# One core, a hybrid encoder layer: the convolution's split halves and the output weights change places in SBUF, with another chunk order and another list of priorities

## The reference, cut to what matters

```
h = rms_norm(x); u = h @ w_in                       # 1024 -> 2560 columns: q, k, v (512 each), conv (1024)
a = neighbourhood_attention(q, k, v, rpb)           # 8 heads x 64, window of rows x 16 columns, relative bias
c = conformer_conv(uc)                              # GLU, depthwise conv of width 31, layer norm, swish
m = concat(rms_norm(a), rms_norm(c))
x = x + m @ w_out                                   # 1024 x 1024
x = x + hier_moe(rms_norm(x))                       # top-1 group of 4, top-2 of 8 experts in it, 32 experts
y = rms_norm(x)
```

## Time and profile before

| | us |
|---|---|
| median of 3 runs | 912.96 (912.54 to 914.18) |
| the profiled execution | 913.56 |
| its span in the trace | 911.7 |

### The profile page before, as it was taken

One profiled execution on the slowest core, in us unless ns is written; L12 is line 12 of the kernel. 1 busy time (PEld: TensorE's weight loads), 2 busy tenths in 40 slices (PEclk: granted clock), 3 DMA queues, 4 the chain that ended last, 5 costly groups with the idle time before them and its releaser, 6 DMA issues.

```text
span 911.7 us, 15694 instructions
## 1 busy us (share of the span) xinstructions
PE 848.1 (93%) x5814; PEld 571.5 (63%) x5815; DVE 374.4 (41%) x697; ACT 242.3 (27%) x482; POOL 139.2 (15%) x288
## 2 busy tenths in 40 slices
PE   3989999999979999989999879999999999999984
PEld 2879977777757878965555445555555555555531
DVE  5399979796374535541111101111111111111146
ACT  5223216545675222101111111111111111111122
POOL 4200010000000001022222111212222212121113
PEclk9998999999979999899999999999999999999997
DMA  7543543413251293959999999999999999999975
GB/s 210 125 91 104 156 162 139 151 47 105 66 166 47 104 401 147 402 214 418 423 418 420 419 419 422 418 420 420 420 420 419 420 420 420 419 414 420 391 290 185
DMA packets 82014, 266.04 MB, mean 292 GB/s; under 512 B 19129, under 2 KB 44985, under 8 KB 57401
## 3 DMA queue, kind: packets, MB, share of 16 engines
q1 hardware_dynamic: 64272, 245.11, 68.9%
q0 software_dynamic: 7888, 18.78, 5.4%
q10 hardware_dynamic: 9816, 1.66, 1.0%
HBM read 247.53 MB, written 27.34 MB: 302 GB/s over the span
## 4 chain that ended last, share of the span: by engine, by line
PE 55%; DMA 16%; SPq 7%; DVE 6%; issue 1%; ACT 1%; POOL 0%; POOLq 0%; DVEq 0%; ACTq 0%
DMA big<-in_w_up 16%; PE ps L1299 14%; PE ps L1336 9%; PE ps L1053 8%; PE ps L1186 7%; SPq L771 7%; PE ps L1302 3%; PE ps L1314 2%; DVE big L1713 2%; PE ps L1290 2%; PE ps L1072 2%; PE ps L1105 1%; PE ps L1084 1%; PE ps L690 1%; PE ps L1205 1%
## 5 line engine op out<-in xcount | busy, mean ns | idle before, releaser
L2026 DVE TENSOR_TENSOR big<-ps,big 64x256 f32<-64x256 f32 x78 | 33.2, 426 | 392.0 <-ACT big L1592 392.0
L1302 PE MATMUL ps<-ring,big 128*64 128x256 f32 x704 | 156.1, 379 | 4.7 <-DMA ring<-in_w_up 4.7
L1299 PE MATMUL ps<-ring,big 128*64 128x256 f32 x704 | 156.4, 379 | 0.9 <-DVE big L2015 0.9
L1053 PE MATMUL ps<-hT,w_split 128*128 128x512 f32 (+1 forms) x768 | 145.7, 345 | 4.1 <-DVE hT L1651 3.6
L1053 PEld LDWEIGHTS ps<-hT,w_split 128*128 128x128 f32 x768 | 118.6, 191 | 26.2 <-issue 11.7
L1299 PEld LDWEIGHTS ps<-ring,big 128*64 128x64 f32 x704 | 96.0, 137 | 56.3 <-issue 12.5
L1302 PE MATMUL ps<-big 128*64 128x256 f32 x544 | 121.5, 380 | 5.1 <-DMA big<-in_w_up 5.1
L1299 PE MATMUL ps<-big 128*64 128x256 f32 x544 | 121.6, 380 | 0.0
L1302 PEld LDWEIGHTS ps<-ring,big 128*64 128x64 f32 x704 | 96.1, 137 | 10.5 <-DMA ring<-in_w_up 6.4
L1299 PEld LDWEIGHTS ps<-big 128*64 128x64 f32 x544 | 73.9, 137 | 39.2 <-issue 9.0
L1592 ACT ACTIVATE big<-ps 64x256 f32<-64x256 f32 x78 | 29.3, 375 | 245.1 <-PE ps L1302 231.7
(11 more groups left out here) (244 smaller groups left out, 1092.5 us busy)
## 6 DMA issues: line engine op xcount, KB each, us to landing
ring<-in_w_gate SPq DMA_DIRECT2D x44, 1024.0 KB, 27.3
ring<-in_w_up SPq DMA_DIRECT2D x44, 1024.0 KB, 28.0
ring<-in_w_down SPq DMA_DIRECT2D x44, 1024.0 KB
big<-in_w_gate SPq DMA_DIRECT2D x20, 1024.0 KB
big<-in_w_up SPq DMA_DIRECT2D x20, 1024.0 KB
big<-in_w_down SPq DMA_DIRECT2D x20, 1024.0 KB
w_raw<-in_w_in SPq DMA_DIRECT2D x20, 512.0 KB, 4.1
results<-spare POOLq DMA_DIRECT2D x12, 512.0 KB, 2.9
```

Of the source, the lines that this page charges most:

```text
L1053: mm = pe.matmul(ps[:, n % 2, 0:size], w_split[:, sub, hi_w, k, :], hT[:, k // 4, hi_h, k % 4, cols], **flags)
L1299: pe.matmul(ps[0:BLK, 6 * h, 0:FH], xT[:, k % (KD // 2), q, :], gate_w[s][:, k, fs], start=(k == 0), stop=(k == KD - 1))
L1302: mm = pe.matmul(ps[BLK:2 * BLK, 6 * h + 1, 0:FH], xT[:, k % (KD // 2), q, :], up_w[s][:, k, fs], start=(k == 0), stop=(k == KD - 1))
L2026: nc.vector.tensor_tensor(hb[:, fs], ps[BLK:2 * BLK, 6 * h + 1, 0:FH], sG[:, fs], ALU.mult).then_inc(hb_ready[h], 1)
```

## The change

The convolution's high part gets a place of its own, `conv_hi`, on the squares `sq` (the start of `mid`), and its low part, `conv_lo`, on the convolution's output `conv_out`, each block over the block that it is made of. `chi` therefore waits for the sum of squares (`ssc_done`) and no longer for the last group of `win`. `wo_split2` and `wo_raw[1]` move to `mT[:, 0]`, the half of h that the convolution's parts leave free; their load and their `whi` wait for the last `win` group and no longer for `ssc_done` and `c_done`. `whi` of chunk 0 waits for all groups but the last two, its `wlo` for all. The first half of the first output product waits for two of four `clo`, the second half for all. SP waits for `wlo` of chunk 2 before the experts' early loads. `asq` gets a wait of its own for `norm`. In `CHUNKS`, ("conv", 3) now comes ahead of ("qk", 0). `FIRST` and `PATIENCE` have new numbers, from which all orders in the planned stage follow.

```diff
-CHUNKS = [("conv", 0), ("conv", 1), ("v", 0), ("v", 1), ("conv", 2), ("qk", 0), ("conv", 3), ("qk", 1), ("qk", 2), ("qk", 3)]
+CHUNKS = [('conv', 0), ('conv', 1), ('v', 0), ('v', 1), ('conv', 2), ('conv', 3), ('qk', 0), ('qk', 1), ('qk', 2), ('qk', 3)]
...
-FIRST = dict(win=50, ht=1, sc=10, tn=8, va=8, inv=7, mean=15, meanb=3, var=2, rows=0, rowsb=0, ssc=3, asum=6, poa=45, po=45, tnh=20, lgt=2,
-             glu=0, lo=1, tap=60, bias=20, sh=5, rinv=4, norm=4, alo=12, wlo=2, xc=4, xcb=4, rstd=0, zn=4, znb=4, clo=1, sscc=0, ssac=2, aad=9, vad=4, cad=3, px=1, h2=0,
-             out=0, hi=1, strip=40, ex=5, tc=3, vo=2, ahi=12, asq=14, sqx=4, silu=0, chi=0, csq=4, whi=3, sq2=0, tch=0,
-             rootl=0, roota=0, rootc=0, root2=0, load=0, rawl=1, wload=2, xload=3, raws=0)
+FIRST = dict(win=34, ht=-2, sc=21, tn=22, va=1, inv=2, mean=12, meanb=0, var=19, rows=16, rowsb=7, ssc=10, asum=11, poa=22, po=22, tnh=2, lgt=23,
+             glu=18, lo=1, tap=18, bias=9, sh=15, rinv=4, norm=20, alo=8, wlo=25, xc=16, xcb=21, rstd=7, zn=17, znb=17, clo=20, aad=17, vad=20, cad=1, sscc=17, ssac=4, px=20, h2=21,
+             out=-7, hi=1, strip=40, ex=21, tc=9, vo=10, ahi=27, asq=24, sqx=0, silu=13, chi=26, csq=16, whi=12, sq2=12, tch=4,
+             rootl=-4, roota=11, rootc=2, root2=14,
+             load=0, rawl=1, wload=23, xload=19, raws=0)
...
-HANDOVER, LANDING, PATIENCE, SWITCH = 0.13, 2.0, dict(DVE=0.25), 1.3
+HANDOVER, LANDING, PATIENCE, SWITCH = 0.13, 2.0, dict(PE=0.1, DVE=0.1, ACT=0.3), 1.3
...
-            middle.enter_context(nc.sbuf_tensor("under_hT", [P, 2 * KD * T], F32R))
+            wo_split2 = middle.enter_context(nc.sbuf_tensor("wo_split2", [P, 2, JC, OUT_COLS], F32R))[:]
+            wo_raw1 = middle.enter_context(nc.sbuf_tensor("wo_raw1", [P, JC, OUT_COLS], F32))[:]
+            middle.enter_context(nc.sbuf_tensor("under_hT", [P, KD * T], F32R))
...
-            middle.enter_context(nc.sbuf_tensor("under_big", [P, JC * OUT_COLS], F32))
-            wo_split.append(middle.enter_context(nc.sbuf_tensor("wo_split2", [P, 2, JC, OUT_COLS], F32R))[:])
-            middle.enter_context(nc.sbuf_tensor("under_mid", [P, MID - 3 * JC * OUT_COLS], F32))
+            conv_hi = middle.enter_context(nc.sbuf_tensor("conv_hi", [P, JC, T], F32R))[:]
+            middle.enter_context(nc.sbuf_tensor("between", [P, 2 * ZW + FW - JC * T], F32))
+            conv_lo = middle.enter_context(nc.sbuf_tensor("conv_lo", [P, JC, T], F32R))[:]
+            middle.enter_context(nc.sbuf_tensor("under_mid", [P, MID - 2 * ZW - FW - JC * T], F32))
...
-                freed, count = ((split_done, RUNS), (ssc_done, 1), (osplit_done, 2), (osplit_done, 1))[n]
+                freed, count = ((split_done, RUNS), (win_done, len(GROUP_AT)), (osplit_done, 2), (osplit_done, 1))[n]
...
+            sp.wait_ge(osplit_done, OUT_CHUNKS - 1)
             sp.wait_ge(wout_done, NT * OUT_CHUNKS // 2)
...
-                        pe.wait_ge(c_done, JC)
+                        pe.wait_ge(c_done, JC // 2)
...
+                elif g == 0:
+                    pe.wait_ge(c_done, JC)
...
-                        mm = pe.matmul(ps[:, OUT_BANK[g], :], mT[:, part, hi_m, k, t * P:(t + 1) * P],
+                        half = mT[:, 1, hi_m] if part else (conv_hi, conv_lo)[hi_m]
+                        mm = pe.matmul(ps[:, OUT_BANK[g], :], half[:, k, t * P:(t + 1) * P],
...
+                act.wait_ge(attn_done, 2 * j + 2)
...
+                if j == 0:
+                    act.wait_ge(ssc_done, 1)
-                nc.scalar.activation(mT[:, 0, 0, j, :], conv_out[:, j, :], ACT.Copy,
+                nc.scalar.activation(conv_hi[:, j, :], conv_out[:, j, :], ACT.Copy,
...
-                if n == 0:
-                    act.wait_ge(win_done, len(GROUP_AT))
-                elif n == 1:
-
-                    act.wait_ge(c_done, JC)
+                if n < 2:
+
+                    act.wait_ge(win_done, len(GROUP_AT) - 2 * (1 - n))
...
+                if n == 0:
+                    dve.wait_ge(win_done, len(GROUP_AT))
...
-                nc.vector.scalar_tensor_tensor(mT[:, 0, 1, j, :], conv_out[:, j, :],
-                                               vec[:, V_GO + JC + j:V_GO + JC + j + 1], fp32(mT[:, 0, 0, j, :]),
+                nc.vector.scalar_tensor_tensor(conv_lo[:, j, :], conv_out[:, j, :],
+                                               vec[:, V_GO + JC + j:V_GO + JC + j + 1], fp32(conv_hi[:, j, :]),
```

More of the change, by code:

```diff
@@ L247, in parts @@
     add(("roota",), [("ssac",)])
-    for n, free in ((0, ("lo", RUNS - 1)), (1, ("ssc",)), (3, ("wlo", 0)), (2, ("wlo", 1))):
+    for n, free in ((0, ("lo", RUNS - 1)), (1, last_group), (3, ("wlo", 0)), (2, ("wlo", 1))):
         add(("wload", n), [free])
@@ L251, in parts @@
         add(("xload", n), [free])
-    for n, free in enumerate((last_group, ("clo", JC - 1), ("va", ASLOTS - 1), ("po", NT - 1))):
+    for n, free in enumerate((("win", len(CHUNKS) - 1, 1, 1), last_group, ("va", ASLOTS - 1), ("po", NT - 1))):
         in_line(("whi", n), [free, ("wload", n)])
-        in_line(("wlo", n), [("whi", n)])
+        in_line(("wlo", n), [("whi", n), last_group])
     for j in range(JC):
@@ L264, in parts @@
         in_line(("silu", j), [("znb", j)])
-        in_line(("chi", j), [("silu", j), last_group])
+        in_line(("chi", j), [("silu", j), ("ssc",)])
         in_line(("clo", j), [("chi", j)])
@@ L281, in parts @@
         if s in (0, HALF):
-            after += [("alo", PAIRS - 1), ("sh", ASLOTS - 1)] if s else [("clo", JC - 1)] + [taker(*g) for g in groups[-2:]]
+            after += [("alo", PAIRS - 1), ("sh", ASLOTS - 1)] if s else [("clo", JC // 2 - 1)] + [taker(*g) for g in groups[-2:]]
         if s == 2:
@@ L287, in parts @@
         in_line(("poa", s), after, line="po")
-        in_line(("po", s), [], line="po")
+        in_line(("po", s), [] if s else [("clo", JC - 1)], line="po")
         in_line(("px", s), [("po", s)] + ([("rootc",)] if s == 0 else [("roota",)] if s == HALF else [])
@@ L460, in encoder @@
             wo_split1 = middle.enter_context(nc.sbuf_tensor("wo_split1", [P, 2, JC, OUT_COLS], F32R))[:]
-            wo_split = [wo_split0, wo_split1]
+            wo_split = [wo_split0, wo_split1, wo_split2]
+            wo_raw.append(wo_raw1)
         mT = hT
@@ L488, in encoder @@
         attn_sq = mid[:, o:o + 3 * T].rearrange("p (b n) -> p b n", b=3)
-        wo_raw.append(mid[:, 0:JC * OUT_COLS].rearrange("p (k n) -> p k n", k=JC))
         h2 = mid[:, 0:NT * D].rearrange("p (t d) -> p t d", t=NT)
```

## The result

The changed kernel takes 905.08 us (median of 4 runs, 902.87 to 907.74); the kernel before took 912.83 beside it (4 runs). The medians are 7.75 us apart, 3.6 less than the 11.4 forecast; the ratio is 0.9909, with an interval of 0.9891 to 0.9927.

What follows compares the result with a forecast made beforehand. PE bounds the kernel until the router (93% busy), then full DMA engines in the experts' loop. Gains 6.9 + 3.2 + 1.8 - 0.5 = 11.4 off 913.56 give 902.2, as a median 901.6; predicted 901.5, range 896.5 to 910.

Steps and rivals of the forecast that it cites:

- The gap only moves: Rival, after the last `win`: first output product still starts at 258 to 260; in all 905 to 906; 12 in 100.
- Place A: From last `win` to first output product: cost 9.7 us, of which 6.9 would be gained, between 3.9 and 9.7.
- The term for the clock after the short gap: After the short wait before the first output product: a low clock costing 1.5 us, between 0 and 3.3.
- neither touched: Before about 250 us: the 2.4 us wait for block 1's `mean` and one near 65 us stay unchanged.
- what would make the forecast wrong: Signs: new PE waits before 252 (`mean`, blocks 2 and 3), a wait at product 12, an earlier router without earlier end.
- Place B: At the first logits: PE's 1.5 us wait for `h2` and 1.7 of low clock go, 3.2 gained, or 0.
- Place C: Tail, last output product to router: six logits run without a gap; 1.8 of 2.7 us gained, between 0 and 2.7.
- Attention: Rival: attention, starting a chunk later, becomes the bound and the kernel gets slower, median 922; 1 in 10.
- The 0.5 set aside for a wait there: Before the second twelve output products: a loss of 0.5 us for late attention or the reloaded x.
- the five table loads between 140 and 165: On ACT: four of five function table loads go, 5.1 us of ACT, worth 0 at the end.
- the 541 of the forecast: From the router to the end: the experts' loop is untouched and takes the same 541 us.

Runs made afterwards that it cites:

- the second profile: The changed kernel run once more, nothing altered, as reference for the follow-up runs: 907.43 us, ratio 0.994; its profiled execution took 906.17.
- the wide tail: The changed kernel plus an unused 512-column product behind each of the tail's first five logits: 903.79 us, ratio 0.9897.
- mean_wr_wide: The changed kernel with later `mean`, router weights scaled early, `lgt=2`, and a wide product behind each of the last two `tnh`: 898.9 us, ratio 0.9836.

## Why the prediction was right, and where it was off

The direction was right, and so were the places where the time comes from; 905.08 lies in the range and 3.6 above the number. It lies outside the forecast's own 898.5 to 904.5 and in the 905 to 906 of the rival *The gap only moves*, whose mechanism did not occur (first product at 255.09, not 258 to 260). So the number alone would have spoken for the wrong story, and the stages have to decide. Up to the router the forecast was 11.4 and the profiled execution gave 6.1. Step by step:

**Place A: right mechanism, undersized.** Forecast +6.9, from 9.7 less 1.3 idle and 1.5 clock. 0.65 of idle time is left, and the clock of 252 to 266 is 1.00: 9.0 gained. `ssc` came at 237.69 (forecast about 240), the first product 2.45 after the last `win` (2.5), chunk 1's `wlo` ran from 261.0 to 263.3 (262), still hidden. The term for the clock after the short gap, between 0 and 3.3, was 0.

**What earns it** I had not separated. I reasoned as if the places and the early `ssc` were needed for nearly all of it. The runs put the orders alone at 0.9957 and the places alone at 1.0032; on top of the orders the places give 2.8 us. The orders win place A's clock: they keep PE fed with attention, so that a gap of 15.7 us costs 4.8 of idle time and no low clock. The places then take the idle time from 4.8 to 0.65. The new places need the orders: without them there is nothing to write early.

**Before 252: the step that said "neither touched" failed.** I had argued that `mean` keeps its rank before `win` and so its single wait. It keeps the rank, but PE now comes to block 2's as well before DVE is done with the block: 2.37 at 160.49. With the old chunk order the second wait is gone, so it comes with the chunk order. This was named among what would make the forecast wrong (for blocks 2 and 3), and not priced. Moving the two `mean` shows that such waits cost what the list says, or nearly: 2 to 4 us for both, less than their 4.8 since 1.9 come back behind them.

**Place B: right.** The wait for `h2` and its clock are gone (1.00 in 328 to 334), 3.2; a wait of 0.7 for `px` in front of a `tnh` is new.

**Place C: the failed term.** Forecast +1.8, a tail of 15.9 us; measured 20.49 and, in the second profile, 21.06. Its order is as forecast (all six logits behind the last product), and the work at full clock is 13.8, even less than the 15.0 that I had. But the sum held that a tail without idle runs at full clock, and the granted clock was 0.67 and 0.65, 6.7 us of the 20.49. Set against the tail of before, with the three logits that were only moved (5.6), it is 12.11 + 5.6 - 20.49 = -2.8. B and C come from the same order of the logits, and together they gave 0.4 where 5.0 was forecast; with the logits back among the products no difference was shown either. That the measured time is only 3.6 off is in part luck: what place A gave beyond its forecast paid for some of this. The sum as measured is 9.0 - 2.4 + 3.2 - 0.7 - 2.8 = 6.3, against 6.1 from the two router times. It leaves out two terms of the stage before 252 that nearly cancel: the profile after has a clock of 0.89 from 110 to 125, behind the first wait for `mean`, where before and in the second profile it is 1.00 (0.11 x 15 = 1.7), and one attention slot fewer lies before 252.

**Attention** did not become the bound: its last `alo` starts at 296.41 after, at 309.28 before, although the first scores came at 164.35 (forecast 161). The 0.5 set aside for a wait there wasn't needed, apart from the 0.7 above. Of the five table loads between 140 and 165 one is left, as forecast, and nothing at the end follows from it. From the router to the end it is 541.31 against 540.98: the 541 of the forecast.

**What stays open.** Two profiles (the orders alone, the logits among products) have 543.1 from the router to the end, where all others have 540.1 to 541.4. The experts' loop is alike for 480 us from the router; the two microseconds arise in the last 40, where PE's clock is lower than after (0.91 and 0.92 against 1.00, then 0.74 against 0.80). Another kernel with 0.92 and 0.74 there took 540.56, so the clock's mean doesn't settle it. PE is busy for 11.1 and 11.2 us in the last 21 in these two, and for 8.0 and 8.6 in the changed kernel and in the wide tail. The cause wasn't tested.

## What to carry to other kernels

When buffers change places to let work start earlier, check in the timeline that the work's input is ready by then, and what the earlier piece is queued ahead of: the places alone made this kernel slower. Judge a gap by the engine's idle time and clock in it, not by when the next stage starts. Where a stage ends in many narrow matmuls, count its time at both levels of the clock, and try both remedies: keep it short by running what you can among wide products, or put a wide one between. And when an effect of a few microseconds is wanted, hold such a stage fixed in both kernels.

## What the runs showed of the hardware

I had taken the clock to fall after waits, as at places A, B and C before. In the tail of the changed kernel it is 0.50 from 348 to 356 and again from 362, with PE and its weight loads busy for all of it, in matmuls of 36 and 128 columns of float32. Between the two it is back at 1.00 (358 to 360), and nothing but the same narrow matmuls runs there or just before: they don't hold it down at all times, and why it comes back is open. With a product of 512 columns after each of five logits it was 1.00 in the tail of all three kernels that had them; with two in a shorter tail (`mean_wr_wide`) it was 0.95. The ends of matmuls are modelled in this profile, so that very short pauses between them can't be excluded. The Trainium skill ("TensorE: Matmul & The Clock Gate", HAM oscillation) has a kernel with short bursts of matmuls lose the clock in its waits for DMA, and (A second HAM failure mode) another kernel by micro-idles while it cycles through PSUM. The first isn't what happened here, as no wait shows in this tail; the second can be neither shown nor excluded.

The tail's clock also differs between executions of kernels with the same tail: 0.67 and 0.65 in two profiles of the changed kernel, 0.80 with only `mean` moved, 0.87 with the old chunk order and 0.92 with the orders alone, that is 21.06 to 15.23 us for the same work. The forecast's 15.9 for this tail was met or beaten in two of these five. The runs of the changed kernel lie 4.9 and 4.1 us apart, those of the later `mean` 9.4, of the old chunk order 3.1 and of the orders alone 1.8; those of the three with the wide tail lie 1.5 to 3.9 apart. That the wide products narrow the spread is therefore not shown in general. With only `mean` moved the time goes with the mean clock of the whole run (896.03 at 0.989, 905.47 at 0.972); in the six runs of the changed kernel's second comparison it doesn't (909.36 at 0.974, but 905.25 and 906.17 at 0.978 and 907.6 at 0.98). So one profiled execution can lie some microseconds from the median, and where it lies is not told by the tail alone.
